# The prompt's compressed branch moved between the convolution tiles of the input projection

## The reference

```
z      = x @ w_in + b_in                       # split: conv b, c, h | q | kv_cmp, kv_sel, kv_win | gates
conv   = b * conv3(c * h)                      # causal, width 3, per channel
o_cmp  = softmax(q kc^T, blocks already past) vc       # kc, vc: an MLP over each block of 64 tokens
o_sel  = softmax(q k_sel^T) v_sel              # only the 16 best blocks
o_win  = softmax(q k_win^T) v_win              # the last 512 positions
o      = g0 * o_cmp + g1 * o_sel + g2 * o_win  # gates g per head and branch
out    = concat(o, conv) @ w_out
```

## Time and profile before

| | |
|---|---|
| median of three runs | 1381.91 us |
| the profiled execution | 1381.58 us |
| its span, first to last instruction | 1379.9 us |
| mean granted clock of PE | 0.977 |
| PE busy | 1292.8 us, 94% |
| DVE, ACT, POOL busy | 760.9, 432.7, 230.1 us |
| chain of work that ended last, by engine | PE 77%, DVE 12%, ACT 5%, issue 3%, DMA 2% |
| the split of one weight tile: ACT high part, DVE low part | 1.05 us, 1.26 us on average |

### The profile page before, as it was taken

One profiled execution on the slowest core, in us unless ns is written; L12 is line 12 of the kernel. 1 busy time (PEld: TensorE's weight loads), 2 busy tenths in 40 slices (PEclk: granted clock), 3 DMA queues, 4 the chain that ended last, 5 costly groups with the idle time before them and its releaser, 6 DMA issues.

```text
span 1379.9 us, 29891 instructions
## 1 busy us (share of the span) xinstructions
PE 1292.8 (94%) x11917; PEld 1180.2 (86%) x11917; DVE 760.9 (55%) x1217; ACT 432.7 (31%) x815; POOL 230.1 (17%) x229
## 2 busy tenths in 40 slices
PE   6999999999999889999989999696999999999996
PEld 5999999999999878999946666595999999999994
DVE  3786477467837764434456666547344443444446
ACT  3222232122312225232245556216422222122224
POOL 0342044114403405000234422000000000000000
PEclk9999999999999999999999999898999999999998
DMA  4787266246526412323277764132423333332211
GB/s 139 204 224 184 63 200 200 62 129 193 177 78 186 143 55 63 65 62 90 85 227 258 231 207 130 40 99 80 154 86 104 102 95 106 106 106 88 94 61 65
DMA packets 215664, 173.95 MB, mean 126 GB/s; under 512 B 22931, under 2 KB 206402, under 8 KB 215172
## 3 DMA queue, kind: packets, MB, share of 16 engines
q1 hardware_dynamic: 209412, 155.64, 38.1%
q0 software_dynamic: 6144, 16.79, 3.6%
HBM read 168.44 MB, written 8.10 MB: 128 GB/s over the span
## 4 chain that ended last, share of the span: by engine, by line
PE 77%; DVE 12%; ACT 5%; issue 3%; DMA 2%; SPq 1%; POOL 0%; DVEq 0%; ACTq 0%
PE ps L757 45%; PE ps L884 8%; PE ps L811 7%; PE ps L781 4%; DVE dlo L1745 3%; PE ps L1240 2%; DVE glo L1740 1%; DMA draw<-in_ffa_down_dram 1%; PE ps L1276 1%; PE ps L1211 1%; ACT ghi L1376 1%; PE ps L1256 1%; ACT xh L1550 1%; ACT x L1550 1%; PE ps L1325 1%
## 5 line engine op out<-in xcount | busy, mean ns | idle before, releaser
L757 PE MATMUL ps<-xh,ghi 128*128 128x272 f32 x1872 | 395.7, 293 | 19.7 <-DVE xl L2010 14.9
L757 PE MATMUL ps<-xl,ghi 128*128 128x272 f32 x1872 | 388.9, 289 | 0.0
L757 PE MATMUL ps<-xh,glo 128*128 128x272 f32 x1872 | 387.5, 288 | 0.0
L757 PEld LDWEIGHTS ps<-xh,ghi 128*128 128x128 f32 x1872 | 300.0, 190 | 36.5 <-issue 18.6
L757 PEld LDWEIGHTS ps<-xl,ghi 128*128 128x128 f32 x1872 | 296.3, 190 | 0.0
L757 PEld LDWEIGHTS ps<-xh,glo 128*128 128x128 f32 x1872 | 295.4, 190 | 0.0
L1740 DVE TENSOR_TENSOR glo<-graw,ghi 128x1024 fp32r<-128x1024 f32 x117 | 147.5, 1261 | 102.2 <-ACT ghi L1376 100.0
L721 POOL COPY perm<-landing 128x1024 f32<-128x1024 f32 x64 | 138.2, 2178 | 305.4 <-DMA landing<-in_cache_cmp_kv_dram 305.2
L1816 DVE SCALAR_TENSOR_TENSOR x<-ps,x 128x544 f32<-128x544 f32 x176 | 126.6, 719 | 105.6 <-PE ps L811 105.0
L1875 DVE SCALAR_TENSOR_TENSOR yt<-ps,yt 128x512 f32<-128x512 f32 x88 | 60.5, 690 | 156.6 <-PE ps L884 156.6
L1376 ACT ACTIVATE ghi<-graw 128x1024 fp32r<-128x1024 f32 x117 | 122.6, 1049 | 28.3 <-PE ps L757 21.9
(11 more groups left out here) (340 smaller groups left out, 1486.6 us busy)
## 6 DMA issues: line engine op xcount, KB each, us to landing
landing<-in_cache_cmp_kv_dram SPq DMA_DIRECT2D x256, 128.0 KB, 2.5
page<-in_cache_sel_kv_dram SPq DMA_DIRECT2D x128, 128.0 KB, 4.8
page<-in_cache_sel_kv_dram POOLq DMA_DIRECT2D x128, 128.0 KB, 5.0
graw<-in_ffa_gate_dram SPq DMA_DIRECT2D x22, 512.0 KB, 4.5
graw<-in_ffa_up_dram SPq DMA_DIRECT2D x22, 512.0 KB, 4.1
draw<-in_ffa_down_dram SPq DMA_DIRECT2D x88, 128.0 KB, 2.6
graw<-in_w_in_dram SPq DMA_DIRECT2D x44, 256.0 KB, 3.3
graw<-in_ffb_gate_dram SPq DMA_DIRECT2D x22, 512.0 KB, 3.8
```

The source lines that it names most:

```text
L757: last = nc.tensor.matmul(out[:, h, 0:HALF], a[:, k, :], b[:, k, h * HALF:(h + 1) * HALF], start=(k == 0 and a is hi and b is xhi), stop=( ...
```

## The change

The steps of the prompt's compressed branch, and the transposes of the new decode tokens' weights, become functions of PE and VectorE. PE runs one in the middle of each of the projection's tiles 14 to 17, 19 and 22; VectorE runs its part after the convolution that goes with the tile; ScalarE copies its half of the scores before the result of tile 16 and takes the exponential after that of tile 17. The branch uses banks 0, 1, 6 and 7, which the projection leaves free. Its output stays in these four banks until ScalarE copies it to `po` after tile 22, in two parts. VectorE scales the first queries before the `ctok` copies. Behind the projection PE keeps the decode tokens' gates (now bank 2), the new tokens' values (bank 3) and the decode sequences' compressed values (bank 4). The attention keeps its order; some of its waits now name the new semaphore counts. The programs of SP and POOL are the same.

```diff
@@ PE
-            for j in range(14, 21):
-                project(j)
+            def prompt_values():
+                pe.wait_ge(q["gates_ready"], 1)
...
+            def prompt_scores():
+                pe.wait_ge(q["vbd_ready"], 1)
...
+            def new_rows():
+                pe.wait_ge(q["selt_ready"], 1)
...
+            def prompt_scores_back():
+                pe.wait_ge(q["spt_by_act"], 1)
+                pe.wait_ge(q["spt_by_dve"], 1)
...
+            def prompt_turned():
+                pe.wait_ge(q["pp_ready"], 1)
...
+            def compressed_out():
+                pe.wait_ge(q["ptp_ready"], 1)
+                pe.wait_ge(q["ctok_ready"], 1)
+                for r in range(R):
+                    last = nc.tensor.matmul(ps[:, (0, 1, 6, 7)[r], :], vbd[:, r, :, :].rearrange("p g d -> p (g d)"),
+                                            ptp[:].rearrange("p t c -> p (t c)"), start=True, stop=True)
+                last.then_inc(q["op_in_psum"], 1)
+
+            project(14, prompt_values)
+            project(15, prompt_scores)
+            project(16, new_rows)
+            project(17, prompt_scores_back)
+            project(18)
+            project(19, prompt_turned)
+            project(20)
             conv_rows()
             project(21)
-            project(22)
+            project(22, compressed_out)
...
@@ PE, scores_p and keys_t
+                if u == 0:
+                    pe.wait_ge(q["op_ready"], 1)
+                if u == 1:
+                    pe.wait_ge(q["gates_ready"], 2)
+                    pe.wait_ge(q["onew_ready"], 1)
...
                 if n == 0 and m == 0:
-                    pe.wait_ge(q["op_ready"], 1)
+                    pe.wait_ge(q["op_ready"], 2)
+                    pe.wait_ge(q["ocs_ready"], 1)
@@ ACT
             for j in range(12, NT):
                 if j + 1 < NT:
                     next_split(j)
+                if j == 16:
+                    act.wait_ge(q["spt_in_psum"], 1)
+                    act.activation(spt[:, 0, :], ps[:, 6, :], ACT.Copy).then_inc(q["spt_by_act"], 1)
                 projected(j)
...
+                if j == 17:
+                    act.wait_ge(q["sp_shifted"], 1)
+                    act.activation(w_cmp, w_cmp, ACT.Exp).then_inc(q["ep_ready"], 1)
             act.wait_ge(q["op_in_psum"], 1)
-            act.activation(po[:], ps[:, 4:8, :], ACT.Copy).then_inc(q["op_ready"], 1)
+            act.activation(po[:, 0:2, :], ps[:, 0:2, :], ACT.Copy).then_inc(q["op_ready"], 1)
+            act.activation(po[:, 2:4, :], ps[:, 6:8, :], ACT.Copy).then_inc(q["op_ready"], 1)
@@ DVE
+            between = {14: prompt_values, 15: prompt_scores, 16: new_rows, 17: prompt_shifted, 18: prompt_weights,
+                       19: prompt_turned}
...
                 if j >= 16 and j < 20:
                     convolved(j - 16)
                 if j == 19:
                     dve.engine_nop().then_inc(q["u_ready"], 1)
+                if j in between:
+                    between[j]()
                 if j >= 20:
                     mixed(j - 20)
             mixed(2)
+            prompt_queries(0)
             dve.wait_ge(q["ctok_in_psum"], 1)
```

More of the change, by code:

```diff
@@ L1131, in _ @@
             project(13, selection_rows)
-            for j in range(14, 21):
-                project(j)
+            def prompt_values():
+                pe.wait_ge(q["gates_ready"], 1)
+                nc.tensor.matmul(ps[0:64, 7, 0:128], rep8[:].rearrange("p x b -> p (x b)"), vcp[:],
+                                 start=True, stop=True).then_inc(q["rep_in_psum"], 1)
+            def prompt_scores():
+                pe.wait_ge(q["vbd_ready"], 1)
+                for g in range(G):
+                    for r in range(R):
+                        last = nc.tensor.matmul(ps[32 * r:32 * r + 32, 6 + g, :], kcp[:, g, :],
+                                                zr[:, r, 0:SEQ], start=True, stop=True)
+                last.then_inc(q["spt_in_psum"], 1)
@@ new lines, in new_rows @@
+            def new_rows():
+                pe.wait_ge(q["selt_ready"], 1)
+                for k in range(4):
+                    last = nc.tensor.transpose(ps[0:NS, 0, k * 128:(k + 1) * 128], pnew[:, k, :], ident[:])
+                last.then_inc(q["pnewt_in_psum"], 1)
+            def prompt_scores_back():
+                pe.wait_ge(q["spt_by_act"], 1)
+                pe.wait_ge(q["spt_by_dve"], 1)
+                for g in range(G):
+                    for t in range(QT):
+                        last = nc.tensor.transpose(ps[:, 6 + g, t * 128:(t + 1) * 128], spt[:, g, t * 128:(t + 1) * 128],
+                                                   ident[:])
+                last.then_inc(q["sp_in_psum"], 1)
@@ new lines, in prompt_turned @@
+            def prompt_turned():
+                pe.wait_ge(q["pp_ready"], 1)
+                for t in range(QT):
+                    last = nc.tensor.transpose(ps[0:64, 6, t * 128:(t + 1) * 128], w_cmp[:, t * 64:(t + 1) * 64], ident[:])
+                last.then_inc(q["ptp_in_psum"], 1)
+            def compressed_out():
+                pe.wait_ge(q["ptp_ready"], 1)
+                pe.wait_ge(q["ctok_ready"], 1)
+                for r in range(R):
+                    last = nc.tensor.matmul(ps[:, (0, 1, 6, 7)[r], :], vbd[:, r, :, :].rearrange("p g d -> p (g d)"),
+                                            ptp[:].rearrange("p t c -> p (t c)"), start=True, stop=True)
+                last.then_inc(q["op_in_psum"], 1)
@@ L1142, in _ @@
             pe.wait_ge(z_out[1], NT // 2)
[L1143 to L1147, removed]
             for k in range(BR * R):
-                last = nc.tensor.matmul(ps[:, 6, k * NS:(k + 1) * NS], gate_sel[k // 8][:, k % 8, :],
+                last = nc.tensor.matmul(ps[:, 2, k * NS:(k + 1) * NS], gate_sel[k // 8][:, k % 8, :],
@@ L1150, in _ @@
                                         zr[0:BR * NH, G0, SEQ:T], start=True, stop=True)
             last.then_inc(q["gates_in_psum"], 1)
-            pe.wait_ge(q["ctok_ready"], 1)
+            pe.wait_ge(q["pnewt_ready"], 1)
+            for k in range(4):
+                last = nc.tensor.matmul(ps[:, 3, k * 128:(k + 1) * 128], pnt[:, k, :],
+                                        kvtok[0:NS, QT, 3 + 2 * (k // 2), :], start=True, stop=True)
+            last.then_inc(q["onew_in_psum"], 1)
@@ L1153, in _ @@
+            pe.wait_ge(z_out[0], NT // 2 + 1)
             for n in range(NB):
-                last = nc.tensor.matmul(ps[32 * (n % 4):32 * (n % 4) + 32, 0, n // 4 * 128:(n // 4 + 1) * 128],
+                last = nc.tensor.matmul(ps[32 * (n % 4):32 * (n % 4) + 32, 4, n // 4 * 128:(n // 4 + 1) * 128],
                                         pct[:, n // 4, 32 * (n % 4):32 * (n % 4) + 32], vc_all[:, n, :],
@@ L1157, in _ @@
             last.then_inc(q["ocs_in_psum"], 1)
[L1158 to L1188, removed]
             def scores_p(u):
@@ L2145, in _, with prompt_values, prompt_scores @@
             dve.tensor_copy(selt[:].rearrange("p n b -> p (n b)"), ps[:, 0, 0:128]).then_inc(q["selt_ready"], 1)
+            def prompt_values():
+                dve.wait_ge(q["rep_in_psum"], 1)
+                dve.tensor_tensor(vbd[0:64], ps[0:64, 7, 0:128].rearrange("p (o g d) -> p o g d", o=1, g=G).broadcast_to(
+                    [64, R, G, HD]), diag[:].rearrange("p r (g o) -> p r g o", o=1).broadcast_to([64, R, G, HD]), ALU.mult
+                    ).then_inc(q["vbd_ready"], 1)
+            def prompt_scores():
+                dve.wait_ge(q["spt_in_psum"], 1)
+                dve.tensor_copy(spt[:, 1, :], ps[:, 7, :]).then_inc(q["spt_by_dve"], 1)
@@ new lines, in new_rows, with prompt_shifted @@
+            def new_rows():
+                dve.wait_ge(q["pnewt_in_psum"], 1)
+                dve.tensor_copy(pnt[:].rearrange("p k r -> p (k r)"), ps[0:NS, 0, :]).then_inc(q["pnewt_ready"], 1)
+            w_p = w_cmp
+            by_row = w_p.rearrange("p (x b) -> p x b", b=8)
+            mx = small[:, C_MX:C_MX + 32]
+            wide = mx.rearrange("p (x o) -> p x o", o=1).broadcast_to([128, 32, 8])
+            def prompt_shifted():
+                dve.wait_ge(q["sp_in_psum"], 1)
+                for g in range(G):
+                    steps(dve.tensor_tensor(
+                        w_p.rearrange("p (t g r b) -> p t g r b", t=QT, g=G, r=R)[:, :, g, :, :],
+                        ps[:, 6 + g, :].rearrange("p (t r b) -> p t r b", t=QT, r=R)[:, :, :, 0:8],
+                        blk_neg[:].rearrange("p t (o b) -> p t o b", o=1).broadcast_to([128, QT, R, 8]), ALU.add))
+                steps.settle()
+                steps(dve.tensor_reduce(mx, by_row, AX, ALU.max)); steps.settle()
+                dve.tensor_tensor(by_row, by_row, wide, ALU.subtract).then_inc(q["sp_shifted"], 1)
@@ new lines, in prompt_weights @@
+            def prompt_weights():
+                dve.wait_ge(q["ep_ready"], 1)
```

(32 more changed lines are left out.)

7 lines of the change are left out of this document (removed).

## The result

The changed kernel took 1391.75 us in the median of seven runs (1386.54 to 1394.34), the kernel before 1381.91 (seven runs); the ratio is 1.006 with a 95% interval of 1.0045 to 1.0076, some 6 to 10.5 us slower. The forecast was 1391.7, by the window's landing. The profiled execution took 1391.18 us (span 1389.5), 9.6 more than that of before.

A forecast was written before the change was run, and what follows sets the result against it. PE is full in the projection; behind it the window's landing, started by tile 22's end, becomes the bound. Tile 22 9.65 later, less 2.3, gives +7.4, plus 2.6 for the restart: +10.0, predicted 1391.7 us, range 1387.0 to 1396.5.

The forecast's parts named there:

- the steps were not free: Rival in the projection: gaps between matmuls take the moved steps, tile 22 ends as before; 1381.9 us, chance 0.07.
- VectorE made PE wait 0.5 us and not 3: Rival in tiles 17 to 19: VectorE becomes the bound and PE waits about 3 us; 1394.6 us, chance 0.11.
- the restart was not free: Rival at the first key transposes: the clock returns at once, so the restart costs nothing; 1389.0 us, chance 0.17.
- the loads were a bound: Rival behind tile 22 claimed the opposite: loads no bound, first transpose 7.0 us earlier; 1374.6 us, chance 0.03.
- The moved work: Six PE steps before tile 22's end: 7.91 of work, 1.14 of breaks, 0.6 of waits, 9.65 us later.
- The waits: PE waiting in the projection: 0.4 us in tile 19 for DVE's softmax, 0.2 in tile 22 for `ctok` copies.
- the values, scores and products: Moved PE steps at full clock: spreading the values 0.36 us, scores 1.85, four output products 3.63.
- The transposes: Moved PE transposes: four of new rows 0.52 us, eight of scores 1.03, four of weights 0.52.
- The landing: Sequence 0's window lands 20.1 us after tile 22, at 710.05, moving the first key transpose by 7.4 us.
- The restart: Attention's start after PE's wait: clock 0.50 for the first 4 to 6 us, costing 2.6 us.
- The worst case of the range: Moved work with PE waiting 3 us in the projection and restarting at the worst: 1395.5 us.
- The rule of the Trainium skill's page: Rival at the attention's restart: transposes don't raise the clock, a whole turn runs at half; 1408.0 us, chance 0.04.

The follow-up runs named there:

- the warm experiment: Changed kernel plus 13 idle products of 512 columns behind the cached values, filling PE's wait for the window; 1387.96 us, ratio 1.0049 to the kernel before.
- the two kernels with few loads: Changed kernel and kernel before, each loading two of sequence 0's 32 pages, sequence 1's loads waiting for sequence 0's window; 1376.26 us (0.9955) and 1381.67 us (1.000).
- with sequence 0 first: Changed kernel, but sequence 1's pages and window are issued only once sequence 0's window has landed; 1386.61 us, ratio 1.003 to the kernel before.
- with the output products behind: Changed kernel with the four output products moved back behind tile 22 instead of in its middle; 1386.94 us, ratio 1.0044 to the kernel before.
- with few loads: Changed kernel loading only two of sequence 0's 32 pages before the attention, sequence 1's loads waiting for sequence 0's window; 1376.26 us, ratio 0.9955 to the kernel before.
- run 24: Not a run's label: in the kernel before, PE had run (executed) 24 products of 24 rows by 32 columns just before the clock fell.

## Why the prediction was right

The direction and its mechanism held, but for the ground of the half clock (below). The loads started 1.0 us behind tile 22, the window's landing took the place of `po`, PE stood idle for 13.96 us, and the clock was at half when it restarted. The rivals fall: the steps were not free (67.17 against 58.51), VectorE made PE wait 0.5 us and not 3, the restart was not free (the warm experiment), the loads were a bound (the two kernels with few loads).

That the forecast lies 0.05 us from the median is in part luck. Of its +10.0 the trace shows +7.5, while the ratio says 6 to 10.5: all three terms came out below what they were put at, and the scatter between executions made up for it. By the terms of the sum:

- The moved work was put at 9.65 and took 8.66. The waits were right (0.6 against 0.5), the values, scores and products too (with their breaks and without waits 6.4 against 6.3). The transposes were mis-sized: I took a row's length, 1.03 for eight, and added 0.19 for the break, but the next product starts before that length is over. In the kernel before it starts at 668.10, 0.79 behind the eight of 667.31 (its row stands below). Sixteen transposes with their three breaks were put at 2.64 and took 0.45 + 0.88 + 0.57 = 1.9. The time from start to start is the price.
- The landing was put at 20.1 behind tile 22 and came at 18.6. I took one execution's figure as a constant; the five kernels that load both sequences side by side show 18.6 to 22.0. The profile of before could have warned that the transfers share: the earlier trace rows gives 9.5 us for half a megabyte.
- The restart was put at 2.6 and took 2.36, with 5.6 us at half clock, as in the earlier trace rows. That the lengths agree is luck in part: with sequence 0 first the same restart was at half for 2.7 us, with the output products behind for 4.3, with few loads for 5.7. And I had tied the half clock to some 15 us of idle time, while the clock had fallen before PE stood idle, and was at half at the restart with 1.1 us of idle time too (few loads). The wait counts in another way: filled with products, it had the clock back before its end.

```profile
668.10 0.49 PE L757 MATMUL ps<-xh,ghi 128*128 128x272 f32 x2
```

The worst case of the range, 1395.5, is more than its terms add up to (1381.58 + 7.91 + 1.14 + 3 - 2.3 + 2.8 = 1394.1); the upper end of the range, 1396.5, is wider by as much.

The rule of the Trainium skill's page "TensorE: Matmul & The Clock Gate", section "Part 4: PE-mode transpose", by which transposes don't count as busy time like other matmuls, did not decide here: the clock came back within the first 5.6 us, made of some 17 key transposes and the score products of one unit. The kernel with sequence 0 first tests the rule itself, and its trace does not agree: there twelve of these fp32 transposes alone brought the full clock back, 2.7 us after the restart. The measurement decides.

What stays open is the scatter of the landing, and the 2 us or so by which executions differ before tile 13 is reached.

## What to carry to other kernels

Before work is moved out of a stretch, find everything that the next stage waits for in it, not the wait that ended last alone: a transfer that starts at the same moment and lands 2 us earlier leaves 2 us to gain at most, whatever is removed. If that transfer is released by the end of the stage into which the work is moved, the move delays it by its full price, and idle time under a transfer is the cheapest place for small steps. Compare traces from a common event just ahead of the change, so that scatter elsewhere does not enter.

## What the runs showed that was not expected

The clock also falls with PE busy. In the kernel before, PE's row is full from 680.3 to 690 and its clock 1.00 until 685, and yet this row of 1 us (columns as above) stands in it:

```profile
686.00:687.00 1.00, 1.00 (x12) 0.48 (x5) 0.42 (x1) 0.00 (x0) 0.64 (x2) 0.50 0.84 243
```

Just before the fall, at about 685.3, PE had run 24 products of 24 rows by 32 columns. The changed kernel's clock fell at 694.9, 1.1 us after the same products, and with few loads at 692.2, before their end; there the new tokens' values (its row at 692.59) took 2.05 us instead of the 1.15 of the earlier trace rows and no gap stood before them. That the small products are the reason is not shown: no run leaves them out.

Half a megabyte landed 7.7 and 7.9 us after its issue (two kernels) when it shared the DMA engines with sequence 0's pages alone, and 8.8 to 11.7 us (five kernels) when 4 MB for the next sequence were issued after it on both queues: what is issued later delays what was issued first. Why it varies so much within that range is not settled.
